# A four-layer float32 decoder on one core: ups by half tokens behind each junction, 512-column ups, and last downs in threes

## The reference, cut to what matters

```python
h = h + rmsnorm(mixer(rmsnorm(h, g0)), g1)
h = h + rmsnorm(ffn(rmsnorm(h, g2)), g3)
```

## Time and profile before

| | us |
|---|---|
| median of 3 runs (lowest, highest) | 1138.71 (1136.61, 1138.85) |
| the profiled execution | 1139.96 |
| its span, first to last instruction | 1138.2 |
| PE busy in it | 1108.5 (97%) |
| DVE, ACT, POOL busy | 737.4, 614.4, 131.5 |
| mean granted clock of PE | 0.995 |

### The profile page before, as it was taken

How to read it: one execution, slowest core, us unless ns; L and a number is a source line. 1 busy time by engine, 2 the same in 40 slices (tenths; PEclk the granted TensorE clock), 3 DMA queues, 4 the chain that set the end, 5 groups by cost and what they waited for, 6 DMA issues and landing times.

```text
span 1138.2 us, 18946 instructions
## 1 busy us (share of the span) xinstructions
PE 1108.5 (97%) x7666; PEld 1018.6 (89%) x7666; DVE 737.4 (65%) x846; ACT 614.4 (54%) x800; POOL 131.5 (12%) x131
## 2 busy tenths in 40 slices
PE   9999999999999999999998999999999999999998
PEld 8979999998999889999987999999799878999996
DVE  6877767667677677766768555555766546555554
ACT  7655655556555565555565444444567865444442
POOL 1011322220012164222110000000000000000000
PEclk9999999999999999999999999999999999999999
DMA  9875455554534365555553455555453324555551
GB/s 346 296 259 186 163 207 184 184 185 148 185 123 163 126 238 179 192 184 184 184 184 112 159 193 184 184 184 184 135 199 111 113 109 165 187 185 184 184 184 37
DMA packets 31126, 201.99 MB, mean 177 GB/s; under 512 B 3640, under 2 KB 3808, under 8 KB 8544
## 3 DMA queue, kind: packets, MB, share of 16 engines
q1 hardware_dynamic: 28032, 189.16, 46.5%
q0 software_dynamic: 3040, 12.07, 3.2%
HBM read 200.15 MB, written 2.63 MB: 178 GB/s over the span
## 4 chain that ended last, share of the span: by engine, by line
PE 81%; DVE 9%; ACT 5%; issue 2%; DMA 1%; POOL 1%; SPq 0%; DVEq 0%; ACTq 0%; POOLq 0%
PE wk L568 17%; PE wk L569 17%; PE wk L570 17%; PE acc L568 8%; PE acc L569 8%; PE acc L570 8%; ACT w_hi L285 2%; DVE w_lo L292 1%; DVE x L1314 1%; DMA raw<-ws 1%; DVE a_lo L1333 1%; POOL o_rs L521 1%; DVE sq L1326 1%; DVE sq L1307 1%; ACT sq L1018 1%
## 5 line engine op out<-in xcount | busy, mean ns | idle before, releaser
L292 DVE TENSOR_TENSOR w_lo<-raw,w_hi 128x2048 fp32r<-128x2048 f32 x173 | 397.0, 2297 | 228.4 <-ACT w_hi L285 228.3
L285 ACT ACTIVATE w_hi<-raw 128x2048 fp32r<-128x2048 f32 x173 | 330.8, 1913 | 315.0 <-PE wk L570 237.5
L568 PE MATMUL wk<-a_hi,w_hi 128*128 128x256 f32 x1472 | 418.3, 284 | 5.5 <-DVE a_lo L1333 5.5
L569 PE MATMUL wk<-a_lo,w_hi 128*128 128x256 f32 x1472 | 417.3, 283 | 0.0
L570 PE MATMUL wk<-a_hi,w_lo 128*128 128x256 f32 x1472 | 417.2, 283 | 0.0
L568 PEld LDWEIGHTS wk<-a_hi,w_hi 128*128 128x128 f32 x1472 | 283.0, 192 | 9.2 <-issue 7.1
L569 PEld LDWEIGHTS wk<-a_lo,w_hi 128*128 128x128 f32 x1472 | 283.0, 192 | 1.6
L570 PEld LDWEIGHTS wk<-a_hi,w_lo 128*128 128x128 f32 x1472 | 283.1, 192 | 0.0
L568 PE MATMUL acc<-w_hi,b_hi 128*128 128x512 f32 x432 | 168.8, 391 | 1.7 <-DVE b_lo L325 1.7
L569 PE MATMUL acc<-w_lo,b_hi 128*128 128x512 f32 x432 | 168.6, 390 | 0.0
L570 PE MATMUL acc<-w_hi,b_lo 128*128 128x512 f32 x432 | 168.1, 389 | 0.0
(11 more groups left out here) (225 smaller groups left out, 1305.9 us busy)
## 6 DMA issues: line engine op xcount, KB each, us to landing
raw<-ws SPq DMA_DIRECT2D x173, 1024.0 KB, 4.8
gain<-gains POOLq DMA_DIRECT2D x13, 512.0 KB, 4.8
raw<-ws SPq DMA_DIRECT2D x8, 256.0 KB, 6.0
region<-rows SPq DMA_DIRECT2D x1, 1664.0 KB, 9.8
lines_dram<-line_dram POOLq DMA_DIRECT2D x1, 1536.0 KB, 10.5
bias<-gains POOLq DMA_DIRECT2D x3, 512.0 KB, 6.5
region<-xT SPq DMA_DIRECT2D x4, 256.0 KB, 4.3
x<-x_rows SPq DMA_DIRECT2D x1, 1024.0 KB, 7.1
```

The source lines that it names most:

```text
L285: act.activation(w_hi[:, u % CUT, :], raw[:, u % RAW, :], ACT.Copy).then_inc(hi_ready, 1)
L292: dve.tensor_tensor(w_lo[:, u % CUT, :], raw[:, u % RAW, :], w_hi[:, u % CUT, :].bitcast(F32), ALU.subtract).then_inc(lo_ready, 1)
L568: pe.matmul(o, still, moving, start=first, stop=False, skip_group_check=True)
L569: pe.matmul(o, still, moving_lo, start=False, stop=False, skip_group_check=True)
```

## The change

- `unit_pair` replaces `unit_feat` for most ups: one matmul with w_hi over 512 columns (a_hi and a_lo are neighbours in one tensor now) and one with w_lo over the 256 of a_hi, which adds to the second half of the bank. The two halves of the bank are summed afterwards: ACT copies the second out, DVE adds the first. An up so takes two banks, and PE waits for the sum one step back. In an MLP the sum is squared on DVE in one instruction.
- `first_ups` and `first_projections`: the first three units behind a junction begin with w_hi alone and tokens 0 to 127 (`half_pair`, `half_token`, 16 matmuls of 256 columns each); then come tokens 128 to 255 and w_lo (`low_pair`, `low_token`).
- `last_downs` takes three pairs. In the junctions after GMLP, FFN0, FFN1 and MLP0 (`by_threes`) half 0 is turned ahead of the third down's second half. `turn_half(n, 1)` stands between the second and third half piece, behind WARM = 12 dummy matmuls; `turn_half(n, 0)` has none.
- The pooling goes by token halves.
- w_hi gets four buffers (HIGH), w_lo keeps three (LOW), LAG is 3, splits are reordered at the junctions, and w_lo of the first unit is made in two halves (`lo_half`).
- All loops are written out. The bias copies are issued between POOL's gates in FFN0.

```diff
-WARM = 36
-LAG = 2
+HIGH, LOW = 4, 3
+WARM = 12
+LAG = 3
...
+            def unit_pair(u, banks):
+                pe.wait_ge(lo_ready, u + 1)
...
+                for k in range(DT):
+                    for m in range(2):
+                        c = slice(m * P, (m + 1) * P)
+                        pe.matmul(banks[:, m, :], wh[:, k, c], a_hl[:, k, :, :].rearrange("p e t -> p (e t)"),
+                                  start=k == 0, stop=False, skip_group_check=True)
+                        mm = pe.matmul(banks[:, m, T:2 * T], wl[:, k, c], a_hi[:, k, :],
+                                       start=False, stop=k == DT - 1, skip_group_check=True)
+                mm.then_inc(unit_done, 1)
...
+            def first_ups(n, u):
+                banks = [up_banks(n, r) for r in range(3)]
+                half_pair(u[0], banks[0], n, 0)
+                if result(n) is wk:
+                    pe.wait_ge(yg_ready, turn(n, 1, 1))
+                    pe.wait_ge(y_squared, turn(n, 1, 1))
+                half_pair(u[1], banks[1], n, 0)
+                turn_half(n, 1)
+                half_pair(u[2], banks[2], n, 0)
+                for r in range(3):
+                    half_pair(u[r], banks[r], n, 1)
+                    low_pair(u[r], banks[r])
...
             def last_downs(n, u, pairs, hidden, res=acc):
+                count = len(pairs)
                 for h in range(2):
-                    for e in range(2):
+                    for e in range(count):
+                        last = e == count - 1
...
+                        if h == 1 and last and by_threes(n) and n != J_MLP1:
+                            turn_half(n, 0)
...
+                if not by_threes(n):
+                    turn_half(n, 0)
...
+            first_projections(J_FFN0, U_DIFF, a_hl, a_hi, a_lo)
+            pe.wait_ge(dv_ready, 2)
+            scores_pair(0)
...
+            pool_map(0)
+            pe.wait_ge(band_ready, 2 * len(WINDOWS))
+            pool_band(0)
+            turn_half(J_FFN1, 1)
+            pool_map(1)
+            pool_band(1)
+            pe.wait_ge(pz_ready, 4)
+            turn_half(J_POOL, 0)
...
                 x_squares(0)
+                if n != J_POOL:
+                    split_hi(act, last + 2)
+                else:
+                    split_hi(act, last + 3)
+                if by_threes(n):
+                    input_hi(0)
                 result_squares(1)
-                input_hi(0)
+                if not by_threes(n):
+                    input_hi(0)
...
                     act.wait_ge(unit_done, u + 1)
+                    if i:
+                        act.wait_ge(s["padded"], 2 * (i - 1) + a + 1)
+                    act.activation(ffn_low[:, a, :, :], ffn_banks(n, i, a)[:, :, T:2 * T], ACT.Copy).then_inc(s["low"], 1)
+                    if i and a == 0:
+                        ffn_hidden(l, base, i - 1)
...
+                if n == J_POOL:
+                    pool_scaled(1)
+                if by_threes(n):
+                    lo_half(dve, last + 1, 0)
                 next_input(0)
...
+                if by_threes(n):
+                    lo_half(dve, last + 1, 1)
+                    input_lo(0)
...
                 new_x(1)
-                input_lo(0)
+                if n == J_FFN1:
+                    pool_scaled(0)
...
-                    dve.wait_ge(unit_done, plus(u + 1, TURN, it))
-                    dve.tensor_copy(hb[:, p + a, :, 2:HW], two(wk[:, p + a, :])).then_inc(s["padded"], 1)
+                    dve.wait_ge(s["low"], 2 * i + a + 1)
+                    dve.tensor_tensor(hb[:, p + a, :, 2:HW], ffn_banks(n, i, a)[:, :, 0:T], ffn_low[:, a, :, :], ALU.add)\
+                       .then_inc(s["padded"], 1)
```

More of the change, by code:

```diff
@@ L265, in build @@
         ffn = [{n: sem(f"ffn{l}_{n}") for n in
[L266 removed]
+                ("pad_zero", "low", "padded", "tap2", "taps", "gelu", "gated", "hid_hi", "hid_lo", "last_gated", "last_lo")} for l in range(2)]
         mlp = [{n: sem(f"mlp{l}_{n}") for n in
[L268 to L273 removed]
@@ L275, in landed, with split_hi @@
-        def landed(eng, u, it=None):
-            eng.wait_ge(raw_landed[u % RAW], plus(16 * (u // RAW + 1), 16 * (TURN // RAW), it))
-        def split_hi(act, u, it=None):
+                ("low", "summed", "square", "hid_hi", "hid_lo")} for l in range(2)]
+        def landed(eng, u):
+            eng.wait_ge(raw_landed[u % RAW], 16 * (u // RAW + 1))
+        def split_hi(act, u):
             if u >= UNITS:
                 return
[L282 to L285, removed]
@@ L555, in _ @@
                     pool.tensor_tensor(b, b, ident[:, :], ALU.subtract).then_inc(band_ready, 1)
-            ffn_phase(1)
+            for i in range(FI - 1):
+                gate_up(pool, 1, i)
             load_gains(J_MLP0)
@@ new lines, in half_there, with half_pair @@
+            def half_there(n, h, k, kv):
+                if k % 4 == 0:
+                    if kv:
+                        pe.wait_ge(blo_ready, 2 * h + k // 4 + 1)
+                    else:
+                        pe.wait_ge(alo_ready, DT + turn(n, h, k // 4))
+            def half_pair(u, banks, n, h, x=a_hl, kv=False):
+                if h == 0:
+                    pe.wait_ge(hi_ready, u + 1)
+                c = slice(h * P, (h + 1) * P)
+                wh = w_hi[:, u % HIGH, :].rearrange("p (k m) -> p k m", k=DT)
+                for k in range(DT):
+                    half_there(n, h, k, kv)
+                    for m in range(2):
+                        pe.matmul(banks[:, m, :].rearrange("p (e t) -> p e t", e=2)[:, :, c], wh[:, k, m * P:(m + 1) * P],
+                                  x[:, k, :, c], start=h == 0 and k == 0, stop=False, skip_group_check=True)
@@ L665, in keep_warm, with turn_half_kv @@
+            def turn_half_kv(h):
+                for f in range(2):
+                    pe.wait_ge(xk_ready, 2 * h + f + 1)
+                    if h and f:
+                        pe.wait_ge(alo_ready, DT + turn(J_MLP0, 1, 0))
+                    for k in range(4):
+                        mm = pe.transpose(turned_kv(h, f)[:, k, :], xk[:, h, f, k * P:(k + 1) * P], ident[:, :])
+                    mm.then_inc(xk_turned, 1)
             def keep_warm(bank, count):
@@ L1358, in junction @@
[L1358 to L1366 removed]
+                    kv_lo(1)
```

660 lines of the change are left out of this document (365 added, 295 removed).

## The result

| | before | changed |
|---|---|---|
| median of the runs | 1138.78 us (1136.61 to 1142.02, 4 runs) | 1122.9 us (1122.63 to 1124.0, 4 runs) |
| profiled execution: time, span | 1139.96, 1138.2 | 1124.0, 1122.1 |
| TensorE matmuls | 7666 | 6474 |

The ratio is 0.9862, with a 95% interval of 0.9846 to 0.9877: the change takes 15.9 us away. 23.7 us were forecast. The time is in the range of 8 in 10 (1104 to 1127), but above the forecast's own range (1108 to 1121). Three terms of the sum behind it are off by over 5 us each: two of them promised too much, one too little.

The account below looks back on a forecast made before the run. The kernel was held bound by PE's stream, except at junctions with 67.0 us without projection work. 12.8 + 4.9 + 0.7 + 3.75 + 2.4 - 1.2 + 0.3 = 23.65 us gave 1115.0, own range 1108 to 1121, 8 in 10 1104 to 1127.

Parts of the forecast that it names:

- The pairs: 512-column ups in unit_pair: a unit falls from 5.76 to 5.56 us, over 64 units 12.8 us saved.
- I take the additive value: In unit_pair, long and short matmuls keep their separate paces, 0.2275 and 0.12 us, when alternated: 5.56 us a unit.
- Rivals 1 and 3: Unit pairs: 1, nothing saved, 1125 us, chance 0.10; 3, short matmul's fixed part hidden too, 1102 us, chance 0.13.
- The junctions: Between phases, token-half chains run under downs and half pieces, cutting time without projection work: 10.85 us saved in all.
- Nothing is added: Split sum on ACT and DVE in FFN and MLP steps: PE's new 16.6 us FFN step leaves 2.1 free, no cost.
- PE waiting on `padded` inside a phase: Named sign of being wrong; the forecast had that sum come 2.4 us after its unit, with 11 us of others between.
- rival 5: A missing unit or input at each junction stalls PE and instruction streaming takes 9.8: 1137 us, no change, chance 0.03.
- The fall behind DIFF: After DIFF's junction PE idles over 4 us and runs at half clock about 3.4 us; 1.5 us charged.
- the row at 948.30: Earlier trace: PE busy 1.73 of 3.40 us, next 3.4 us at clock 0.50, about 1.5 us lost; basis for clock charges.
- Rival 2: The clock falls at all junctions, with 12 warm matmuls for 36: + 9 us, 1124, chance 0.13.
- Rival 4: In ffn_step the ACT-DVE-ACT chain becomes the bound, slower than before: a 19 us step gives 1153 us, chance 0.05.
- The cost of unrolled code: Written-out loops, PE's weight loads waiting on "issue": taken as 0, bounded by 9.8 us lost.

Follow-up runs that it names:

- experiment 1: Changed kernel with each 512-column matmul of unit_pair split back into two of 256: 1130.71 us, ratio 0.9924, 7.3 slower than the changed kernel.
- experiment 2: Changed kernel with all 16 long matmuls of a unit ahead of its 16 short ones: 1117.9 us, ratio 0.9811, 5.5 faster.
- Experiment 5: Changed kernel with the first half's input turned behind the third down, ScalarE and VectorE order following: 1135.95 us, ratio 0.9968, 12.1 slower.
- experiment 4: Changed kernel with the second half's turn ahead of the first-half pieces (MLP0's order kept) and 36 warm matmuls for 12: 1133.2 us, ratio 0.9945, 9.8 slower.
- experiment 8: Changed kernel with VectorE's w_lo splits at DIFF, pool and sticks ahead of the second half's input_lo: 1119.09 us, ratio 0.9822, 4.7 faster.
- experiments 9 and 10: Changed kernel with splits moved behind sums: 9, fourth unit's behind each phase's first sum, 1122.46 us; 10, first FFN steps' behind the next sum, 1126.11 us.
- Experiment 6: Changed kernel with warm matmuls at DIFF, pool and sticks behind the first turn (32, 24, 32), none ahead of the second: 1117.63 us, ratio 0.9812.
- experiment 11: Changed kernel with long matmuls first, warm matmuls behind the first turn, and VectorE's and ScalarE's splits moved at half junctions: 1107.45 us, ratio 0.9718.

## Why the prediction was right in sign and too large

**The pairs: 12.8 forecast, 7.5 found.** The step that failed is "I take the additive value, since the switch between the two forms in the trace costs nothing extra". That switch stood in the trace where a down follows an up, 42 times from long to short and 47 times back, and never in alternation. One by one the long matmul takes 0.236 in place of 0.2275, 0.13 us a unit, and the short ones give back 0.05. 64 units that are just under 0.12 shorter are 7.5 us, and experiment 1 has 7.3 for the same. With the two forms apart (experiment 2) a unit takes the forecast 5.56, and 5.5 us more come in. The mechanism of a fixed part was right, then, and one row for its size was missing. Rivals 1 and 3 each had one of the two bounds; the truth lies 40% of the way to rival 1.

The runs give 7.3 us for 1024 matmuls fewer, 7 ns each, and 12.8 us with the forms apart, 12.5 ns each. The formula that spoke against this edit (the Trainium skill, "TensorE: Matmul & The Clock Gate", "Back-to-back issue gap", 2.5 ns a matmul) would have had 2.6 us. The page gives it for a matmul in isolation and says itself that it does not fit a stream of weight loads and matmuls, which this kernel is; the prediction left that out. The runs disagree with it in both orders.

**The junctions: 10.85 forecast, 15.9 found.** By the timelines, the time without projection work, with what the low clock cost in it, fell as follows (found to some 0.3 us each).

| | GMLP | FFN0 | DIFF | FFN1 and pool | MLP0 | STICK |
|---|---|---|---|---|---|---|
| forecast | 4.9 | 0.7 | -1.2 | 2.4 | 3.75 | 0.3 |
| found | 5.8 | 2.0 | -0.8 | 3.1 | 4.8 | 1.0 |

The single events came as told: a stall of 1.03 ahead of GMLP's downs (1.05), a wait ahead of the first scores (1.00 for 1.8), the end stalls of 0.64 (0.9), 2.59 and 2.84 at band 1 and behind it (3.5 for the first), the low clock behind DIFF, in the pool and behind the sticks. I was off on the same side each time. Behind GMLP the first turn with its wait takes 1.39 us (1.6 booked) and the second with its warm matmuls 2.49 (87.93 to 90.42; 3.3 booked): the second half's input is there when the 12 warm ones end, and no wait is left. Experiment 5 shows what the early input is worth, 12.1 us, about three quarters of the whole gain; the overlay of pieces on the second half's chain is worth 9.8 (experiment 4). Together that is more than the 15.9, so the two are not independent. No run separates the fourth w_hi buffer, LAG = 3, the pool by halves or the written-out loops.

**The phases' first steps: nothing forecast, 7.3 lost.** "Nothing is added", I wrote of the split sum, and weighed its queue only in the steady step. At the start of a phase the same low copy and sum stand behind three or four splits. MLP0: 1.88 us of waiting and 1.6 of low clock, by experiment 8 the result of a transfer that starts late because w_lo of the unit before is late. FFN1: 0.18 + 1.38. FFN0: about 0.6. These rows name 5.6 us. Of the rest, some 0.04 us stand in each down of an FFN step (5.50 for 5.46), and about 1 us has no place that I can name. Two new orders (experiments 9 and 10) did not take FFN1's share away. Two of the prediction's lines had this in sight: PE waiting on `padded` inside a phase stood there as a sign of being wrong, and it came; and rival 5 had a stall at each junction, though for w_lo and far larger.

The three together: 7.5 + 15.9 - 7.3 = 16.1, the difference of the two spans; the 7.3 is what the two other terms leave of it, and the rows bear out 5.6. Two errors of 5 us cancelled, which was luck; the missing 7.3 is what is left.

**The clock: right in place, too low once.** The fall behind DIFF was told as 3.4 us, and it lasted 6.8 (the row at 395.80). The stretch in front of it, 1.84 us busy of 3.40 with transposes in it, is the twin of the row at 948.30; PE also idles on into the fall, until 398.05. Low-clock stretches were four (one of them double), besides one behind the last matmul, with the one of MLP0 that I had not seen. Rival 2, a fall at all junctions, did not come: there is none at the junctions behind GMLP, FFN0 and MLP0. Experiment 6 shows that warm matmuls in this idle time, and not behind the pieces, keep the clock behind DIFF and the sticks; none stand in the idle time inside the pool, and its fall stays.

The prediction read the row at 948.30 as if such a stretch brought the fall. The traces don't bear that out. Before the change, behind FFN0 (first two rows), and in the changed kernel behind the pool (last two), PE had worked as little or less, and the clock stayed:

```profile
284.68:288.08 3.40, 1.73 (x12) 1.00 (x11) 2.41 (x5) 3.33 (x5) 1.13 (x2) 1.00 0.00 0
288.08:291.48 3.40, 3.40 (x28) 3.40 (x29) 3.40 (x3) 3.09 (x3) 0.00 (x0) 1.00 0.85 299
```
```profile
612.40:615.80 3.40, 0.56 (x6) 0.35 (x4) 2.97 (x6) 3.01 (x9) 0.00 (x0) 1.00 0.00 0
615.80:619.20 3.40, 3.40 (x29) 3.40 (x30) 2.04 (x5) 0.30 (x1) 0.53 (x1) 1.00 0.02 5
```

The first row has the same 12 matmuls, 8 of them transposes, and the same 1.73 us as the one at 948.30. So the places that the prediction named were partly luck: a stretch of little work went ahead of each fall, but it does not tell whether one comes.

**What did not come.** Rival 4, the FFN's chain as the bound: PE is busy for all 16.79 us of a step, DVE for 13.50. The cost of unrolled code: PE runs at one pace through the steps, and its matmuls wait on "issue" once, 0.8 us, as before the change.

## What to carry to other kernels

Fewer, longer matmuls save a fixed part of about 12.5 ns each here where equal forms stand together, and 7 ns one by one: put at least two of a form side by side. When a step gets a new hand-over, price it in the first steps behind a junction too, where the splits of several units queue on the same engines, and follow the buffer that they hold to the transfer that it delays. Put the warm matmuls into the gap in which PE stands still, and move the late engine's long operations into the time in which it waits for PE's turn; the four edits of experiment 11 were nearly additive, 16.8 us of 18.5.

## What the runs showed of the hardware

- Behind a 512-column matmul between two 256-column ones the next starts 0.236 us later, in a row of its kind 0.2275; a 256-column one there takes 0.117 in place of 0.120. Two and two, the long ones take 0.233 and the short ones 0.115, and the sum is nearly that of separate rows (a unit 5.64, 5.57, 5.555 us). The cause is open.
- Ahead of the falls at 395.80 and 638.10, and of the one in the earlier trace rows, PE had 1.84, 1.52 and 1.73 us of work in 3.40 (transposes, or the last pieces before a wait). Equal or less work was also followed by no fall (1.73 us from 284.68 before, 0.56 us from 612.40 after). The fall was double (6.8 us) at 395.80, where the idle time ran on into it.
